# Two mixers: merge and output projection in one call, and a norm that runs by token tile beside the last output units

## What is computed

```
merged = gate_a * (o_a @ w_up_a) + gate_b * (o_b @ w_up_b)     # first block
x = x + g_mix * (merged @ w_out)
h2 = modulate(rms_norm(x, norm_ffn_g), sh_ffn, sc_ffn)         # into router and experts

merged = sigmoid(za) * y_a + sigmoid(zr) * y_r                  # second block
h = h + merged @ w_mix_out
x = rmsnorm(h, g_ffn)                                           # into the PEER layer
q = x @ w_peer_q
```

## Time and profile before

| | |
|---|---|
| median of 3 runs | 3625.94 us (3611.97 to 3627.86) |
| profiled execution: its own time | 3627.58 us |
| its span, first to last instruction | 3625.8 us |
| mean granted TensorE clock | 0.958 of full speed |
| first mixer's merge and output projection | 518 to 639 us |
| first norm, to the router's first product | 639 to 660 us |
| second mixer's merge and output projection | 2213 to 2337 us |
| second norm, to the peer projection's first product | 2337 to 2361 us |

### The profile page before, as it was taken

One profiled execution on the slowest core, in us unless ns is written; L12 is line 12 of the kernel. 1 busy time (PEld: TensorE's weight loads), 2 busy tenths in 40 slices (PEclk: granted clock), 3 DMA queues, 4 the chain that ended last, 5 costly groups with the idle time before them and its releaser, 6 DMA issues. The chain is left out here.

```text
span 3625.8 us, 46823 instructions
## 1 busy us (share of the span) xinstructions
PE 3344.4 (92%) x17961; PEld 2831.5 (78%) x17961; DVE 2561.6 (71%) x3642; ACT 1798.0 (50%) x2366; POOL 1121.1 (31%) x665
## 2 busy tenths in 40 slices
PE   7999789799999999995997999799999999899999
PEld 5987567577787887874776766789999998777787
DVE  3463554788888998985336835369988886778886
ACT  3332542478888888885222323234348873233332
POOL 0000300268877777770000000001013333344440
PEclk9999999899999999997998969899999999999999
DMA  5443012477777787773221201326558989999996
GB/s 190 141 164 131 25 65 81 183 254 245 257 250 249 257 272 262 249 241 121 93 74 39 77 7 59 134 69 219 194 205 302 355 344 384 369 360 359 376 359 226
DMA packets 257566, 747.02 MB, mean 206 GB/s; under 512 B 52576, under 2 KB 108656, under 8 KB 222912
## 3 DMA queue, kind: packets, MB, share of 16 engines
q1 hardware_dynamic: 176112, 570.77, 43.6%
q0 software_dynamic: 81232, 173.25, 14.7%
HBM read 793.57 MB, written 110.65 MB: 249 GB/s over the span
## 5 line engine op out<-in xcount | busy, mean ns | idle before, releaser
L1910 DVE TENSOR_TENSOR w_lo<-w_raw,w_hi 128x2048 fp32r<-128x2048 f32 x285 | 652.3, 2289 | 102.1 <-ACT w_hi L1760 98.1
L2949 POOL DMA_INDIRECT rows<-in_peer_u_rows,row_at x128 | 174.0, 1359 | 1277.8 <-DVE row_at L3125 852.1
L1760 ACT ACTIVATE w_hi<-w_raw 128x2048 fp32r<-128x2048 f32 x288 | 551.5, 1915 | 26.9 <-DMA w_raw<-in_e_w,over_rows 25.3
L1406 PE MATMUL ps_peer<-peer_xT_hi,w_hi 128*128 128x384 f32 x1024 | 354.0, 346 | 11.7 <-DVE w_lo L3040 11.7
L3040 DVE TENSOR_TENSOR w_lo<-w_raw,w_hi 128x2048 fp32r<-128x2048 f32 x128 | 293.0, 2289 | 99.2 <-ACT w_hi L2960 98.7
L600 DVE TENSOR_TENSOR w_lo<-w,w_hi 128x1024 fp32r<-128x1024 f32 (+5 forms) x138 | 172.8, 1263 | 268.5 <-ACT w_hi L586 267.4
L586 ACT ACTIVATE w_hi<-w 128x1024 fp32r<-128x1024 f32 (+5 forms) x138 | 148.8, 1088 | 400.2 <-DMA w<-in_w_in 224.7
L2102 PE MATMUL ps_gu<-w_hi,h2T_hi 128*128 128x512 f32 x792 | 320.5, 405 | 26.2 <-DVE w_lo L1910 23.6
L1407 PE MATMUL ps_peer<-peer_xT_lo,w_hi 128*128 128x384 f32 x1024 | 344.6, 336 | 0.0
L1408 PE MATMUL ps_peer<-peer_xT_hi,w_lo 128*128 128x384 f32 x1024 | 344.1, 336 | 0.0
L1406 PE MATMUL ps_peer<-w_hi,coef_hi 128*128 128x512 f32 x768 | 302.1, 393 | 26.4 <-DVE w_lo L3040 23.3
(11 more groups left out here) (539 smaller groups left out, 8235.0 us busy)
## 6 DMA issues: line engine op xcount, KB each, us to landing
w_raw<-in_e_w SPq DMA_DIRECT2D x195, 1024.0 KB, 6.4
w_raw<-in_peer_u SPq DMA_DIRECT2D x64, 1024.0 KB, 6.2
w_raw<-in_peer_v SPq DMA_DIRECT2D x64, 1024.0 KB, 8.9
w<-in_w_in SPq DMA_DIRECT2D x60, 512.0 KB, 4.8
acts<-act_out SPq DMA_DIRECT2D x64, 384.0 KB, 7.2
gates<-gate_tile SPq DMA_DIRECT2D x6, 4096.0 KB, 17.7
gates_back<-gates SPq DMA_DIRECT2D x16, 1536.0 KB, 16.0
act_back<-acts SPq DMA_DIRECT2D x64, 384.0 KB, 10.6
```

The source lines that it names most:

```text
L1406: nc.tensor.matmul(out, w_hi, x_hi, start=first, stop=False)
L1760: nc.scalar.activation(w_hi[:, slot(n), :], w_raw[:, slot(n), :], ACT.Copy).then_inc(hi_done.sem, 1)
L1910: nc.vector.tensor_tensor(w_lo[:, slot(n), :], w_raw[:, slot(n), :], w_hi[:, slot(n), :].bitcast(F32), ALU.subtract).then_inc(lo_done.sem, 1)
L2949: nc.gpsimd.indirect_dma_start(out=row(i), out_offset=None, in_=src, in_offset=bass.IndirectOffsetOnAxis(ap=row_at[:, which, k:k + 1], axi ...
```

## The change

Merge and output projection become one call of `project` with twelve blocks: the 4-chunk branch first in both mixers, then the 8-chunk branch, then four output blocks of 256 columns. Three things are new in it.

`made` (class `Made`) names the merged rows, which come into being in the call: ACT and DVE split them two chunks at a time behind the evictions of blocks 4 to 7, and PE waits for chunk k ahead of the products that read it. `tail` (class `Tail`) is the norm: for the four token tiles of the last output block, ACT takes squares and root, DVE the reciprocal and the scaling, PE eight transposes into four PSUM banks of their own (`ps_turn`), and ACT and DVE evict four squares each with gain and shift. PE makes tile 0's transposes ahead of the last unit and the others behind it. `normalise` and `norm_turned` are gone.

On SP, the router tables and the second norm's gain row are fetched behind output block 1 (`"sp": {9: ...}`), the expert weights and the store of `x` at the head of the experts' block (all in one loop, the store behind the second weight), the second store of `x` behind the last output eviction, and the first three peer weights behind block 3 of the peer projection.

```
+class Made:
+    def __init__(self, x, first):
+        self.x, self.first, self.kc = x, first, x.raw.shape[1]
...
+class Tail:
...
+    def turn(self, pe, t, ps):
+        pe.wait_ge(self.normed.sem, self.b_norm + t + 1)
+        if t >= 2:
+            pe.wait_ge(self.out_dve.sem, self.b_dve + t - 1)
+            pe.wait_ge(self.out_act.sem, self.b_act + t - 1)
+        for k in range(KD):
+            last = self.core.nc.tensor.transpose(ps[:, t % 2 * 2 + k // 4, k % 4 * P:(k % 4 + 1) * P],
+                                                 self.xn[t][:, k * P:(k + 1) * P], self.core.ident[:])
+        last.then_inc(self.turned.sem, 1)
+    def square(self, act, t):
+        nc.scalar.activation(self.xn[t], self.x[:, t, :], ACT.Square, accum_out=stat[:, 0, t:t + 1]) \
+            .then_inc(self.squares.sem, 1)
+        act.wait_ge(self.varied.sem, self.b_var + t + 1)
+        nc.scalar.activation(stat[:, 2, t:t + 1], stat[:, 1, t:t + 1], ACT.Sqrt).then_inc(self.root.sem, 1)
...
+    def scale(self, dve, link, t):
+        dve.wait_ge(self.squares.sem, self.b_sq + t + 1)
+        nc.vector.tensor_scalar(stat[:, 1, t:t + 1], stat[:, 0, t:t + 1], 1.0 / D, EPS, ALU.mult, ALU.add) \
+            .then_inc(self.varied.sem, 1)
+        dve.wait_ge(self.root.sem, self.b_root + t + 1)
+        link(nc.vector.reciprocal(stat[:, 0, t:t + 1], stat[:, 2, t:t + 1]))
+        nc.vector.tensor_scalar(self.xn[t], self.x[:, t, :], stat[:, 0, t:t + 1], None, ALU.mult) \
+            .then_inc(self.normed.sem, 1)
...
 def project
+    made_at = {made_from - made.kc // 2 + i: (2 * i, 2 * i + 1) for i in range(made.kc // 2)} if made else {}
...
+            if tail and tail.store:
+                unit_out(sp, len(units) - 1)
+                tail.store(sp)
...
+                        if opens and b == made_from:
+                            pe.wait_ge(x_lo_done.sem, b_xl + b_made + i // 3 + 1)
...
+                if tail and n >= rows_at + 2:
+                    tail.turn(pe, n - rows_at - 2, ps_turn)
+            if tail:
+                tail.turn(pe, T - 2, ps_turn)
+                tail.turn(pe, T - 1, ps_turn)
...
             for b in range(len(blocks)):
+                if b + 1 == made_from:
+                    for n, k in zip(units_of(b), made_at[b]):
+                        if name == "dve":
+                            unit(n)
+                        for at in ((k,) if name == "act" else made_at[b - 1] if k % 2 == 0 else made_at[b]):
+                            halve_made(at, n)
+                        if k % 2 == 0:
+                            halve_block(b + 1, 0)
+                            halve_block(b + 1, 1)
+                    continue
...
+                for k in made_at.get(b if name == "act" else b - 1, ()):
+                    if b < made_from:
+                        halve_made(k, units_of(b)[-1])
...
+            def high_made(k, n):
+                unit_out(act, n)
+                nc.scalar.activation(made.x.hi[:, k, :], made.x.raw[:, k, :], ACT.Copy).then_inc(x_hi_done.sem, 1)
...
+            def behind_unit(t, link):
+                if t == T - 1:
+                    tail.turned_dve(dve, 1, ps_turn)
+                tail.scale(dve, link, t)
+                if t == T - 2:
+                    tail.turned_dve(dve, 0, ps_turn)
+                if t == T - 1:
+                    tail.turned_dve(dve, 2, ps_turn)
+                    tail.turned_dve(dve, 3, ps_turn)
...
 def first_mixer
-    ring = Ring(core, KD * 512)
+    ring = Ring(core, KD * 256)
...
-            ring.begin(sp, [dram_rows(a["w_up_a"], b * 256, (b + 1) * 256) for b in range(2)])
+            ring.begin(sp, [dram_rows(a["w_up_b"], b * 256, (b + 1) * 256) for b in range(2)])
...
+    out_blocks = [(dram_rows(a["w_out"], b * 256, (b + 1) * 256),
+                   [tokens_unit(merged, KD, toks(t), 256, "dve", residual(t, slice(b * 256, (b + 1) * 256)))
+                    for t in range(T)]) for b in range(4)]
...
+    merge(core, gb, ga, (near, 4, a["w_up_b"]), (gated, KD, a["w_up_a"]), merged, ring, out_blocks, (), tail,
+          {"sp": {9: [fetch_router]}})
...
 def experts
+        for n in first:
             w, part = units[n]
             row = 0 if w == 0 else 1 + order[w - 1][1]
             sp.dma_start(w_raw[:, slot(n), :], a["e_w"][row, part]).then_inc(w_in[slot(n)].sem, 16)
+            if n == 1:
+                sp.dma_start(scratch["x_kept"].rearrange("(t p) d -> p t d", p=P), x[:]).then_inc(x_kept.sem, 16)
...
 def merge
-    project(core, blocks, () if halved else [h1, h2], ring=ring, then=then, second_from=4)
+    project(core, blocks + out_blocks, () if halved else [h1, h2], side, ring, then, 4,
+            Made(merged, len(blocks)), tail)
...
 def peer
+    def fetch_first(sp, ready):
+        for n in range(NW):
+            fetch_weights(sp, n)
+        sp.wait_ge(x_kept.sem, x_kept.at(16))
```

More of the change, by code:

```diff
@@ L473, in project @@
+def project(core, blocks, halve=(), side=None, ring=None, then=(), second_from=0, made=None, tail=None):
     nc = core.nc
@@ L1366, in first_mixer @@
     core.drop(ws, wo, bs, otT, v)
-    out_blocks = [dram_rows(a["w_out"], b * 512, (b + 1) * 512) for b in range(2)]
-    merge(core, ga, gb, (gated, KD, a["w_up_a"]), (near, 4, a["w_up_b"]), ring, out_blocks)
-    core.drop(u, onT, gb)
-    merged = Halves(core, ga, "merged")
     def residual(t, sl):
@@ L3316, in build @@
         experts(core, a, keep, scratch)
-        ring = second_mixer(core, a, keep)
+        ring = second_mixer(core, a, keep, scratch)
         peer(core, a, keep, scratch, out, ring)
```

234 lines of the change are left out of this document (112 added, 122 removed).

## The result

The changed kernel took 3597.01 us (median of 6 runs, 3577.62 to 3609.41), the kernel before, on the same chip, 3624.41 (6 runs, 3604.14 to 3627.86): a ratio of 0.9929, 95% interval 0.9901 to 0.9958. The forecast was 3596, with faster by over 0.5% as the likeliest. The profiled span is 3597.4 us for 3625.8, 28.4 less.

The account below looks back on a forecast made before the run. PE, busy 92% of the span, was taken to be held by engine handover chains at each mixer's junction and norm. First mixer 12.5 plus second 18.9 made 31.4 us off 3627.6: 3596, range 3583 to 3611.

Parts of the forecast that it names:

- junction, first mixer: Between last merge product and first output product, first mixer: 9.5 us of pause and slow products shrink to a 0.4 wait, +9.1.
- junction, second: Same place in the second mixer: 8.3 us of pauses and slow products shrink to a 0.4 wait, +7.9.
- width: First mixer's output units: eight of 512 columns become sixteen of 256, 43.6 us of products become 46.1, −2.5.
- merge order: pause, merge: First mixer, 4-chunk branch first: shorter first weight halves save 1.0 us; the step to the 8-chunk branch costs 0.8.
- norm, first: First mixer, last output product to router's first: serial tile chains of 3.8 us each, 14.5 us for 21.2, +6.7.
- late expert weights: Head of experts' block: third weight, behind the store of x, lands at 17 to 18 us; −1, bounds 0 and −7.
- norm, second: Second mixer, last output product to peer projection's first: tiles of 3.35 us, 13.3 us for 24.3, +11.0.
- scalings at 2.9: Sign of being wrong: DVE's scalings in the last output block spaced at PE's 2.9 us instead of 3.8 and 3.35.
- covered more deeply: Rival for norm and junctions: tile chains keep PE's pace of 2.9 and the clock stays up; 11 us more, 3585; chance 0.14.
- transfers ate nothing: Rival: third expert weight holds ACT 7 us and each tile takes 5; gain falls to 14.0, time 3614; chance 0.15.
- stall at block boundaries: Rival: ACT waiting for evictions stalls each of 22 block boundaries; at 2.3 us each the kernel takes 3647; chance 0.03.
- tile 0 was in time: Rival: PE waits for late tile 0 before the last unit; 3 us late in both mixers gives 3602; chance 0.08.

## Why the prediction was right

The mechanism was as described: both junctions lost their pause and their slow products, and the norms shrank to the tiles' chain. That the time came within 1 us of 3596 is luck: single executions of the changed kernel lie between 3577.62 and 3609.41, and the stretches saved 1.6 us more than the sum while other stages took 4.6 longer. Term by term, in the profiled execution:

| term | predicted | measured |
|---|---|---|
| junction, first mixer | +9.1 | +8.8 |
| junction, second | +7.9 | +7.7 |
| width | −2.5 | −2.5 |
| merge order: pause, merge | +1.0, −0.8 | +1.0, −1.5 |
| norm, first | +6.7 | +6.7 |
| late expert weights | −1.0 | 0 |
| norm, second | +11.0 | +12.3 |
| second merge | 0 | +0.6 |
| sum | 31.4 | 33 |

- *Junctions.* Right. A wait of 0.4 was left for chunk 7; PE lost 0.64 there: output blocks of 47.57, less 0.85 of transposes, less 46.08 for 384 products of 0.12.
- *Width.* 46.1 us for 43.5, as worked out; by an estimate from the cycle counts that the Trainium skill gives, TensorE: Matmul & The Clock Gate, section "Back-to-back issue gap", the term would have been −0.5; the trace disagrees with that again.
- *Merge order.* The pause was right to 0.1. The merge itself lost 1.5 instead of 0.8: 0.8 at the step between the branches, as said, the rest at the merge's start, where 12 steps were at the lower clock for 9 before. Left out was what the order is for: the joined call needs it, 3.3 us.
- *Norm chain.* The tile pace was mis-sized: 3.4 us instead of 3.8 and 2.9 instead of 3.35, because a step starts about when the one before it ends by its printed length, without a hop of 0.1. That gave the chain 10.8 us behind the last product instead of 11.1, and 7.9 instead of 9.1. In the first mixer the way from there to the router's first product was 2.8 instead of 2.5, and the two errors cancel in +6.7. The text named scalings at 2.9 as a sign that the chain is hidden; in the second mixer they stood at 2.9 and were not hidden: DVE's eviction followed the scaling at once. The sign to look for was DVE's idle time behind PE, which shows only in the kernel with the squares ahead.
- *The second mixer's hole.* The sum had it right as a whole, since it was measured against the old hole, but its parts were wrong: 1.0 for the store's wait, the rest for the norm. The runs show 3.5 for the store, the block of its own and the slow transposes together, and 8.7 for the tiles.
- *Late weights.* The weight landed 16.7 us after its stage's start (15.3 after its own issue), where the text took 17 to 18. ACT waited 2.28, over the 1 us that the text had named as a sign of being wrong, but inside the 2.5 that it took for slack, and no time came of it. What was missing is that the slack depends on the router's clock. In DMA: Bandwidth & Descriptors, section "Queues, rings and completion order", the Trainium skill has one ring's descriptors start in order, by which 2 MB and the store's 2 MB stand ahead of it; with that, 5 MB at 0.33 MB a microsecond make 15, an estimate. The trace agrees on the order (the two weights ahead, the store and this weight land 4.8, 8.6, 13.7 and 15.3 us after their issues at 647.08, 647.47, 647.94 and 648.41, one behind the other) and roughly on the time.
- *Rivals.* The tiles' chains were not covered more deeply, transfers ate nothing, PE did not stall at block boundaries beyond the known 0.8, and tile 0 was in time.

## What to carry to other kernels

Where an operand is made by the call ahead, join the calls and split it chunk by chunk behind the evictions that make it, and give the blocks in which that happens enough PE time to cover it. A norm at the end of a product can run by row tile behind it; then the pace of its chain against the unit's time and the order of evictions on DVE decide, and squares that don't need the last columns belong ahead. Before a hole is put down to its longest chain, look whether a transfer ends it: in the second mixer of the kernel before, 1.7 us less of work changed nothing. And a late transfer that costs nothing can cost again once what hid it gets faster, as the third expert weight did.

## What the runs showed of the hardware

The granted clock ahead of the same router products, with PE idle for 3.28 us both times, was low in the kernel before (14 slow steps) and full in the joined call without tiles, and over all profiles 0 to 14 steps were slow, up to 2.8 us. The Trainium skill says the same in TensorE: Matmul & The Clock Gate, section "Part 1: The HAM clock gate": the number of slow products at a start varies from run to run. With work that nothing reads in the idle time just ahead there were 3 slow steps, and none where the idle time left was 0.43 us. Ahead of tile 3's transposes, idle times of 1.7 to 2.9 us gave the lower clock in 11 of 14 cases, and 1.3 us or less in none of 8.

In 14 kernels whose experts' stage is the same but for a few instructions and the place of one transfer, that stage took 969 to 993 us, and six executions of the changed kernel lie 32 us apart: effects of 10 us and less are read from stretches, not from totals.
